# One hybrid decoder layer on one core: the page loop written out behind the q, k, v projection, pages in rings with a wait for each page, the memory projections moved into the loop's first chunks, and each prompt unit spread over three chunks

## What is computed

```python
def sb_block(z, mask, v, carry):
    log_om = jnp.where(mask, jax.nn.log_sigmoid(-z), 0.0)
    suffix = lax.cumsum(log_om, axis=3, reverse=True) - log_om + carry[..., None]
    a = jnp.where(mask, jnp.exp(jax.nn.log_sigmoid(z) + suffix), 0.0)
    o = jnp.einsum("bhqk,bkhd->bqhd", a, v.astype(jnp.float32))
    return o, carry + jnp.sum(log_om, axis=3)
...
    q, k, v, bg, u = mixer_inputs(yp, g_mix[l], w_in[l])
    attn = sb_attention_prompt(q, k, v, sb_bias[l])
    u_ext = jnp.pad(u, ((0, 0), (CONV_K - 1, 0), (0, 0)))
    yp = mixer_output(yp, attn, bg, causal_conv3(u_ext, w_conv[l]), g_attn_out[l], g_conv_out[l], w_out[l])
    mk, mv = memory_kv(mem_prompt, g_mem[l], w_ck[l], w_cv[l])
    yp = cross_attention(yp, mk, mv, g_ca[l], w_cq[l], w_co[l])
    yp = swiglu_ffn(yp, g_ffn[l], w_gate[l], w_up[l], w_down[l])
```

## Time and profile before

| | |
|---|---|
| median of 3 runs | 1239.15 us (1235.28 to 1242.31) |
| profiled execution | 1243.84 us, its span 1242.2 us |
| TensorE busy | 1117.2 us (90%) |
| VectorE, ScalarE, GpSimd busy | 629.9, 393.2, 405.8 us |
| HBM read, written | 206.18 MB, 5.80 MB |
| DMA queues of SP, GpSimd | 139.09 MB, 67.13 MB |

### The profile page before, as it was taken

The page is one execution under the profiler, slowest core; times in us unless marked ns, Lnnn a source line. Parts: engine busy times, 40 slices in busy tenths (PEclk is TensorE's granted clock), DMA queues, the critical chain, the costliest instruction groups (busy, mean ns, idle before and its releaser), DMA issues.

```text
span 1242.2 us, 27559 instructions
## 1 busy us (share of the span) xinstructions
PE 1117.2 (90%) x10055; PEld 1019.4 (82%) x10055; DVE 629.9 (51%) x890; ACT 393.2 (32%) x609; POOL 405.8 (33%) x327
## 2 busy tenths in 40 slices
PE   6999998789688888889789887899999999999997
PEld 5999997666466666666579865899999999999996
DVE  4214954555455554555579544954455001554444
ACT  6212123345354444445451344322121111211111
POOL 2333334243323333333333101342423334242331
PEclk8999999899899889899999999899999999999999
DMA  6222225899989989989954031322221332322222
GB/s 224 85 85 69 84 85 179 304 372 370 341 283 355 332 298 386 345 302 361 306 191 149 1 112 58 102 94 77 68 93 51 101 94 69 101 68 76 64 64 76
DMA packets 125012, 213.49 MB, mean 172 GB/s; under 512 B 9855, under 2 KB 68412, under 8 KB 124894
## 3 DMA queue, kind: packets, MB, share of 16 engines
q1 hardware_dynamic: 101962, 139.09, 33.4%
q0 software_dynamic: 20480, 67.13, 15.2%
q10 hardware_dynamic: 2452, 5.80, 1.3%
HBM read 206.18 MB, written 5.80 MB: 171 GB/s over the span
## 4 chain that ended last, share of the span: by engine, by line
PE 66%; SPq 10%; issue 7%; DMA 6%; DVE 6%; ACT 3%; POOL 1%; DVEq 0%; ACTq 0%; POOLq 0%
PE ps L460 50%; DMA k_page<-in_cache_sb_k 6%; SPq L562 5%; PE ps L1432 5%; SPq L568 4%; PE ps L526 4%; PE ps L301 2%; DVE h_lo L362 1%; DVE r_sum L623 1%; PE ps L1453 1%; POOL w_lo L415 1%; ACT prob L649 1%; DVE r_sq L618 1%; PE ps L1490 1%; DVE xT L613 0%
## 5 line engine op out<-in xcount | busy, mean ns | idle before, releaser
L415 POOL TENSOR_TENSOR w_lo<-w_raw,w_hi 128x2048 fp32r<-128x2048 f32 (+3 forms) x66 | 267.8, 4060 | 547.6 <-ACT w_hi L391 481.4
L460 PE MATMUL ps<-h_hi,w_hi 128*128 128x288 f32 x1216 | 264.8, 300 | 15.4 <-DVE h_lo L362 12.4
L460 PE MATMUL ps<-h_lo,w_hi 128*128 128x288 f32 x1216 | 263.2, 298 | 0.0
L460 PE MATMUL ps<-h_hi,w_lo 128*128 128x288 f32 x1216 | 262.6, 298 | 0.0
L568 POOL DMA_DIRECT2D v_page<-in_cache_sb_v x256 | 137.7, 538 | 260.7 <-issue 199.5
L391 ACT ACTIVATE w_hi<-w_raw 128x2048 fp32r<-128x2048 f32 (+3 forms) x62 | 106.5, 1721 | 365.2 <-PE ps L460 333.4
L460 PEld LDWEIGHTS ps<-h_hi,w_hi 128*128 128x128 f32 x1216 | 198.8, 192 | 17.1 <-issue 9.3
L460 PEld LDWEIGHTS ps<-h_lo,w_hi 128*128 128x128 f32 x1216 | 198.7, 191 | 0.0
L460 PEld LDWEIGHTS ps<-h_hi,w_lo 128*128 128x128 f32 x1216 | 198.5, 191 | 0.0
L1432 PE MATMUL ps<-cc,k_page 128*128 128x128 f32 x1024 | 145.2, 305 | 53.2 <-DMA k_page<-in_cache_sb_k 31.2
L1432 PEld LDWEIGHTS ps<-cc,k_page 128*128 128x128 f32 x1024 | 129.7, 157 | 69.1 <-DMA k_page<-in_cache_sb_k 35.1
(11 more groups left out here) (230 smaller groups left out, 1396.0 us busy)
## 6 DMA issues: line engine op xcount, KB each, us to landing
k_page<-in_cache_sb_k SPq DMA_DIRECT2D x256, 256.0 KB, 5.3
v_page<-in_cache_sb_v POOLq DMA_DIRECT2D x256, 256.0 KB, 5.4
w_raw<-in_w_in SPq DMA_DIRECT2D x12, 1024.0 KB, 5.1
w_raw<-in_w_gate SPq DMA_DIRECT2D x11, 1024.0 KB, 5.3
w_raw<-in_w_up SPq DMA_DIRECT2D x11, 1024.0 KB, 5.3
w_raw<-in_w_down SPq DMA_DIRECT2D x8, 768.0 KB, 4.4
w_raw<-in_w_down SPq DMA_DIRECT2D x8, 640.0 KB, 4.0
w_raw<-in_w_out SPq DMA_DIRECT2D x4, 1024.0 KB, 6.0
```

Source lines behind the costliest of these rows:

```text
L415: return nc.gpsimd.tensor_tensor(w_lo[s][:, ks, :], w_raw[s][:, ks, :], w_hi[s][:, ks, :].bitcast(F32), ALU.subtract)
L460: op = nc.tensor.matmul(ps[:, 2 * t + hf, 0:b - a], weights[s][:, k, t * P:(t + 1) * P], x[:, k0 + k, a:b], start=begin and k == ks[0] and ...
```

## The change

Five things change.

1. The groups are no longer a loop with a register but written out on every engine, so the copies of q, k and v to a fixed place go, and the operands are read where they lie.
2. K pages lie in one ring of 8 slots (16 before), V pages in one ring of 16. Every page load waits for the use of its own slot, and TensorE waits for two pages at a time.
3. The stages `ck` and `cv` go. K pages and the memory weights are loaded behind the last `in` weights. Memory product tiles 0 and 1 stand ahead of chunk 0, tiles 2 to 7 in chunks 0, 2 and 3, the row transposes of their results in chunk 4, and their stores on ScalarE's queue in chunk 4.
4. Prompt unit u has its scores in chunk u + 5, now behind the sample scores, and its transposes and sums two chunks later. The 16 units so lie in chunks 5 to 22.
5. The high and low parts of the conv half of the `out` operand get buffers of their own (`c_hi`, `c_lo`). They lie where two of the samples' memory V are loaded to, and SP waits for the last `out` tile before these loads.

```diff
-            for name in ("inb", "in", "ck", "cv"):
+            for name in ("inb", "in"):
                 load_stage(sp, name)
             sp.wait_ge(s_pt, 16)
...
-            with sp.Fori(0, GROUPS) as g:
-                for c in range(CP):
-                    load_pages(sp, g, c, ck, k_page, s_kp, s_ktr, 8)
-            sp.wait_ge(m_["pv"], 8 * GROUPS + 1)
+            def load_memory_weights(i):
+                if i < 2:
+                    sp.wait_ge(s_wlo, SLOT0["ck"] + i - 1)
+                else:
+                    sp.wait_ge(s_mem_tile, 2 * i - 2)
+                src = views["ck" if i < 2 else "cv"][:, :, (i % 2) * SLOTW:(i % 2 + 1) * SLOTW]
+                sp.dma_start(mw_raw[i % 2][:, :, :], src).then_inc(s_full[i % 2], 16)
+
+            k_pages(sp, 0)
+            load_memory_weights(0)
+            load_memory_weights(1)
+            for C in range(1, CHUNKS):
+                k_pages(sp, C)
+                if C in (1, 2):
+                    load_memory_weights(C + 1)
+            sp.wait_ge(s_mem_tile, 8)
+            sp.wait_ge(s_out, 16 * 5)
             load_stage(sp, "out")
...
             for b in range(BS):
                 load_mem(cmk, b, smk_tok[b]).then_inc(s_cmk, 16)
+            sp.wait_ge(s_tile["out"], 4 * PAIRS["out"])
             for b in range(2):
                 load_mem(cmv, b, smv_tok[b]).then_inc(s_cmv[0], 16)
             load_stage(sp, "cq")
```

The loads of pages (`k_pages` on SP, `v_pages` on GpSimd's queue):

```diff
+        def load_page(eng, C, q, cache, slot, loaded):
+
+            n = 64 * (C // 8) + 32 * (q // 4) + 28 - 4 * (C % 8) + q % 4
+            page = eng.value_load(ptb[0:1, n:n + 1], min_val=0, max_val=N_POOL - 1)
+            eng.dma_start(slot, cache[0, bass.ds(page, 1)].rearrange("o p h d -> p o (h d)")).then_inc(loaded, 16)
+
+        def k_pages(sp, C):
+
+            for q in range(8):
+                if C:
+                    sp.wait_ge(s_ktr, 8 * C + q - 7)
+                load_page(sp, C, q, ck, k_page[:, q:q + 1, :], s_kp[q // 2])
+
+        def v_pages(pool, C):
+
+            for q in range(8):
+                slot = 8 * (C % 2) + q
+                if C >= 2:
+                    pool.wait_ge(s_vsum, 8 * C + q - 15)
+                elif slot >= 11:
+                    pool.wait_ge(s_kv_out, 16 * 4)
+                load_page(pool, C, q, cv, v_page[:, slot:slot + 1, :], s_vp[slot // 2])
```

On ScalarE, VectorE and TensorE (P0 is 5):

```diff
             def group(g, last):
                 for c in range(8):
+                    C, u = 8 * g + c, 8 * g + c - P0
+                    sample_sigmoids(9 * g + c + 1, SEQ)
+                    if 3 <= u < 19 and c:
+                        prompt_out(u - 3)
+                    if C + 1 < CHUNKS:
+                        copy_k(C + 1)
+                    copy_weights(9 * g + c + 1, False)
+                    if 2 <= u < 18:
+                        copy_prompt_weights(u - 2)
+                    if 0 <= u < 16:
+                        prompt_sigmoids(u)
+                    if C in (0, 1):
+                        memory_hi(C + 2)
+                    if C == 4:
+                        memory_rows((0, 2, 4))
+                        store_memory()
...
+                    weights(9 * g + c + 1, 19 * g + 3 + 2 * c, SEQ)
+                    if C in (1, 3, 4):
+                        evac_memory((3, None, 5, 7)[C - 1])
+                    if C + 1 < CHUNKS:
+                        copy_k(C + 1)
...
+                    if 2 <= u < 18:
+                        copy_prompt_weights(u - 2)
+                    if 1 <= u < 17:
+                        prompt_weights(u - 1)
...
+                    if C + 1 < CHUNKS:
+                        k_transposes(C + 1)
+                    if C in (0, 2, 3):
+                        memory_tile((2, None, 4, 6)[C])
+                    if C == 4:
+                        memory_rows((0, 1))
+                    weight_transposes(9 * g + c + 1, 4, u - 2)
+                    if 2 <= u < 18:
+                        prompt_transposes(u - 2)
                     if c < 7:
-                        scores(g, c + 1)
+                        scores(C + 1)
                     elif not last:
-                        new_scores(g, 8)
-                    sums(g, c)
-                    if c % 2 == 1:
-                        prompt_sums(g, c // 2)
+                        new_scores(g + 1)
+                    if C in (0, 2, 3):
+                        memory_tile((3, None, 5, 7)[C])
+                    if C == 4:
+                        memory_rows((2, 3, 4))
+                    if 0 <= u < 16:
+                        prompt_scores(u)
+                    sums(C)
+                    if 2 <= u < 18:
+                        prompt_sums(u - 2)
```

More of the change, by code:

```diff
@@ new lines, in _ @@
+            split_stage(act, "in", between=lambda: tr_copy(act, even(U_M)), after=bias_and_memory)
+            copied(act, U_M[-1])
+            act.wait_ge(s_sum["conv"], 1)
+            hi_parts(act, "ck", mT, G_MEM, range(KD))
+            memory_hi(0)
+            memory_hi(1)
+            rms_root(act, "conv", rstd_c[:, :], T, CH)
+            nc.scalar.preload_act_table(ACT.Sigmoid)
+            tr_copy(act, even(U_VT))
+            tr_copy(act, even(U_KT))
+            copied(act, U_KT[-1])
@@ new lines, in group @@
+                    weights(9 * g + c + 1, 19 * g + 3 + 2 * c, SEQ)
[3 more added lines that the diff above has]
+                        copy_k(C + 1)
+                    if c == 7 and not last:
+                        queries(g + 1)
+                    if C in (0, 2, 3):
+                        evac_memory((2, None, 4, 6)[C])
+                    if C < 2:
+                        conv_root(C)
@@ L1279, in group @@
                         op = nc.vector.tensor_copy(
-                            pT[64 * h2:64 * h2 + 64, T_A:T_A + HP, bass.ds(g * 16 + (SEQ + 8 * s), 8)],
+                            pT[64 * h2:64 * h2 + 64, T_A:T_A + HP, SEQ + 16 * g + 8 * s:SEQ + 16 * g + 8 * s + 8],
                             rows[:, :, 16 * s + 8 * h2:16 * s + 8 * h2 + 8])
                 op.then_inc(m_["rows_copied"], 1)
-                if not last:
-                    fix_values(g, 8)
-            queries(0, 0)
-            fix_values(0, 0)
+            queries(0)
             weights(0, 0, NS)
-            copy_k(0, 0)
-            with dve.Fori(0, GROUPS - 1) as g:
-                group(g, False)
-            group(GROUPS - 1, True)
+            lo_parts(dve, "ck", mT, G_MEM, range(KD))
+            copy_k(0)
+            evac_memory(0)
+            evac_memory(1)
+            for g in range(GROUPS):
+                group(g, g == GROUPS - 1)
             grant(s_free["out"], 2)
@@ L1380, in _, with memory_tile @@
             tr_pe(pe, U_KT)
-            pe.wait_ge(s_op["ck"], KD)
-            gemm(pe, "ck", m_hi, m_lo, NMEM)
-            pe.wait_ge(s_evac["ck"], 1)
-            tr_pe(pe, U_MK[0:3])
-            gemm(pe, "cv", m_hi, m_lo, NMEM)
-            pe.wait_ge(s_evac["cv"], 1)
-            tr_pe(pe, U_MK[3:5])
-            def prompt_scores(g, qb):
-                if qb == 0:
-                    pe.wait_ge(p_["qk_fixed"], g * 2 + 2)
+            def memory_tile(j):
+                i, t = divmod(j, 2)
+                if t == 0:
+                    pe.wait_ge(s_wlo, SLOT0["ck"] + i + 1)
+                if j == 0:
+                    pe.wait_ge(s_op["ck"], KD)
+                    copied(pe, U_KT[-1])
+                if j == 1:
+                    pe.wait_ge(s_rt["conv"], 1)
+                if j >= 2:
+                    pe.wait_ge(s_mem_free, j - 1)
+                for k in range(KD):
+                    for w, (weights, x) in enumerate(((mw_hi, m_hi), (mw_hi, m_lo), (mw_lo, m_hi))):
+                        op = nc.tensor.matmul(ps[:, 5 + 2 * t, 0:NMEM], weights[i % 2][:, k, t * P:(t + 1) * P], x[:, k, :],
+                                              start=k == 0 and w == 0, stop=k == KD - 1 and w == 2)
+                op.then_inc(s_mem_tile, 1)
@@ L1520, in group @@
                 if not last:
-                    new_transposes(g, 8)
-                    scores(g, 8)
-                    new_sums(g, 8)
-            new_scores(0, 0)
-            k_transposes(0, 0)
-            new_transposes(0, 0)
-            scores(0, 0)
-            new_sums(0, 0)
-            with pe.Fori(0, GROUPS - 1) as g:
-                group(g, False)
-            group(GROUPS - 1, True)
-            pe.wait_ge(p_["out_copied"], 4 * GROUPS + 1)
+                    weight_transposes(9 * g + 9, 1, u - 1)
+                    scores(8 * g + 8)
+                    new_sums(g + 1)
+            new_scores(0)
+            k_transposes(0)
+            memory_tile(0)
+            copied(pe, U_KT[-1])
+            weight_transposes(0, 1, 0)
+            scores(0)
+            memory_tile(1)
+            new_sums(0)
+            for g in range(GROUPS):
+                group(g, g == GROUPS - 1)
+            pe.wait_ge(p_["out_copied"], 4 * GROUPS)
             gemm_out(pe)
```

494 lines of the change are left out of this document (234 added, 260 removed).

## The result

The kernel after takes **1260.2 us** (median of 4 runs, 1256.07 to 1261.32) and the kernel before 1240.63 beside it (4 runs). The ratio is 1.0162, 95% interval 1.0128 to 1.0197: slower by 1.6%, where 1228 us, faster, was forecast. The profiled execution took 1256.07 us (span 1254.4), 12.2 us more than the profiled execution of before.

What follows compares the result with a forecast made beforehand. DMA engines were taken as full for part of a group and starved otherwise, with TensorE stalled by late K copies. Terms -23.3 + 12.2 + 8.2 - 18.8 - 1.8 + 12 = -11.5: 1232 us profiled, 1228 median; own range 1215 to 1241, eight-in-ten 1197 to 1255.

Steps and rivals of the forecast that it cites:

- entry, to chunk 0: Ahead of the page loop: the first chunk is entered at 215 us instead of 238.5, -23.3 us.
- chunks 0 to 4: Start of the loop: six memory tiles and five row transposes but no prompt work, 62 us instead of 54.7.
- chunks 5 to 20, with the stores: Prompt work in each chunk and late K copies: 12.7 us a chunk, 212 against 204 us, plus 4.6 for stores.
- chunks 21 to 31: Mostly chunks without prompt work, pages loading at 387 GB/s: 108.5 us against 127.3, -18.8 us.
- tail of the loop: After chunk 31 no prompt unit is left to transpose and copy: -1.8 us.
- `cq` weights and all behind: Query weights' load stands behind the last output tile's wait on SP; TensorE sits 14 us and starts slow: +12 us.
- Rival 2: Eight-slot K ring too short, deciding from landings of 7.4 us on: slower, 1259 us or up to 1320; chance 0.18.
- Rival 1: Overlap works fully: chunks 5 to 20 take 10.9 us instead of 12.7, 29 us less, about 1199; chance 0.20.
- The sign I named for rival 2: Waits for k_page over 25 us in chunks 5 to 20 would show the prediction wrong.
- The stores: In chunk 5 ScalarE issues five stores before the sample sigmoids: 4.6 us charged with their waits.

Runs made afterwards that it cites:

- Experiment 3: The kernel after with 16 K page slots instead of 8 from chunk 6 on: ratio 1.0056 to the kernel before.
- Experiment 7: The kernel after without the 16 prompt attention units: 1249.36 us (ratio 1.0076 to before) with 8 K slots, 1214.84 us (0.9791) with 16 from chunk 6 on.
- experiment 6: The kernel after with prompt sigmoids behind the next chunk's sample sigmoids and 12 K slots from chunk 6 on: ratio 0.9857 to the kernel before.
- Experiment 11: The kernel after with cq weights first, 16 K slots, sigmoids behind, and the last two memory weight slots' low parts on VectorE instead of GpSimd: ratio 0.9758 to before.
- experiment 4: The kernel after (8 K slots) with ScalarE's prompt sigmoids moved behind the next chunk's sample sigmoids: ratio 1.0138 to the kernel before.
- experiment 5: The kernel after with both 16 K slots from chunk 6 on and prompt sigmoids behind the next sample sigmoids: 1221.88 us, ratio 0.9854 to the kernel before.
- experiment 8: The kernel after with the five memory row stores on SP behind chunk 6's K pages instead of on ScalarE in chunk 4: ratio 1.0173 to the kernel before.
- experiment 9: The kernel after with cq weights first, 16 K slots, sigmoids behind: 1209.85 us, ratio 0.9747 to before; with the five stores on SP too, 0.9746.
- experiment 2: The kernel before with only the wait for the last output tile put ahead of the memory V and cq weight loads: 1254.81 us, ratio 1.0102 to before.
- experiment 1: The kernel after with the cq weights' load put ahead of the wait for the last output tile on SP's queue: 1249.76 us, ratio 1.0043 to before.

## Why the prediction was wrong

By its own terms, with the profiled executions (before, after):

| term | predicted | measured |
|---|---|---|
| entry, to chunk 0 | -23.3 | -22.5 |
| chunks 0 to 4 | +7.6 | +16.1 |
| chunks 5 to 20, with the stores | +12.8 | +11.1 |
| chunks 21 to 31, to the end of the last sums | -18.8 | -4.1 |
| tail of the loop | -1.8 | -0.1 |
| `cq` weights and all behind | +12 | +11.7 |
| sum | -11.5 | +12.2 |

The forecast median was 32.5 us too low. 23.7 of them are in the table; the other 8.8 come from how the profiled execution stood to the median: 4.7 us above it before, 4.1 below it after. I had taken the same 4.7 off both. Two slips of arithmetic change nothing: 12.7 x 16 is 203.2, not 203.6, and 0.16 + 0.12 is 0.28, not 0.27.

**The step that failed is that of chunks 21 to 31**, "29.4 MB, at 387 GB/s 76 us": 14.7 us of the 23.7. The rate of the earlier trace rows had been reached with 16 K slots, and I carried it over to a ring of 8. Page waits in the second half of the transposes held these chunks to 353 GB/s (timeline of TensorE in after, chunk 26):

```profile
563.07 1.09 PE L1495 MATMUL ps<-cc,k_page 128*128 128x128 f32 x8 [1.14 <-DMA k_page<-in_cache_sb_k]
566.53 1.85 PE L1495 MATMUL ps<-cc,k_page 128*128 128x128 f32 x8 [2.36 <-DMA k_page<-in_cache_sb_k]
```

Experiment 3 shows how much of it is the ring: with 16 slots and nothing else changed these chunks take 113.0 us instead of 123.2, where 108.5 were predicted. That is 10.2 of the 14.7 us; for the other 4.5 no run has a cause. Experiment 7 shows the same of the ring without prompt work. **Rival 2 had the right mechanism** at 0.18 and came within about a microsecond of the time, 1259, but that is luck: its sum put the loss into chunks with landings of 10 us and more. The landing of a K page from 331 to 600 us was 5.9 us in the median with 8 slots and no prompt work, 11.4 at the longest. Its floor, 5.3 us plus the landing, is 11.2 us by the median; measured were 12.2, two group ends among them, and in single chunks anything from 9.3 to 17.3, so it is no floor for each chunk. The ring costs time at landings below the 7.4 us that I gave. As I read it, a chunk waits for the latest of its pages, and a ring without spare slots can't make a late page good; the lower clock behind each wait, which the sum did not have, comes on top. With 12 slots most of the waits are gone (experiment 6). The Trainium skill ("DMA: Bandwidth & Descriptors", Queues, rings and completion order) has each DMA engine go round-robin between the queues that have work for it. That was no reason against the rival: K and V landed equally fast (5.4 and 5.3 us in the page of after), and the loss comes from when a load may be issued, on which the rule is silent.

**Chunks 0 to 4, +8.4 us more than predicted.** Chunk 2 took 20.5 us instead of 15.4, chunk 1 10.1 instead of 8. I had no term for page waits among four loads of memory weights of 1 MB on the same queue, nor for the stopped scans, nor for the clock behind a wait. In chunk 2 of after TensorE waits 1.3 us for a page and 2.4 for a K copy that stands behind the stopped scan; from 247 to 253 the granted clock is then 0.53, and 16 transposes take 3.65 us where they take 2.03. Experiment 11 takes the stopped scans away and the time stays; page waits are what is seen in their place. That the weights' loads cause them was not tried, so this part stays argued.

**Chunks 5 to 20 were right** in time (216.6 us predicted with the stores, 215.1 measured), in the waits for the kT copies (22.5 us on VectorE and 4.2 on ScalarE between 286 and 500; some 30 predicted) and in their cause, which experiments 4 and 5 show. But they did not show what a cure is worth. Rival 1 gave 29 us for full overlap; with 8 slots the moved sigmoids were worth 0.002, with 16 slots 0.020 of the time, 25 us. The sign I named for rival 2, page waits over 25 us in these chunks, did not appear: the late copies hid the late pages. There were none between 286 and 500 us in after, and 13.9 us once the copies came earlier (experiment 4). It was a bad sign to name.

**The stores** were charged 4.6 us. Chunk 5 does last 15.1 us, with 4.2 us of waits, and with the stores off ScalarE and the long ring chunk 5 is 4.8 us shorter, so the charge was of the right size. On SP they cost as much again in late K pages (experiments 8, 9); whether another place would give it back is open.

**The tail** brought nothing: from the end of the last sums to the output product it is 3.75 us (3.86 before). The last weight transposes still wait 1.73 us and the group's rows still go through VectorE (1.39); so it seems that the removed prompt unit stood beside these; no run tests it.

**The `cq` weights** were right: gap 14 predicted, 15.6 measured, and by the ratios the time moved by 12.7 and 14.8 us in experiments 2 and 1. The landing was 7.3 us (685.69 to 693.01) for the 6.8 of the earlier trace rows.

## What to carry to other kernels

When one wait is shortened or hidden, ask which wait lies under it: neither TensorE's late copies nor the short ring showed its price alone (0.002 and 0.011), and the two edits together gave 0.031. Here 12 slots did what 16 did and 8 did not, at median landings of 5 to 6 us: size a ring by the lead time of its last slot against the latest landing, not the median, and don't carry a rate over that was measured with a deeper ring; leaving the work out altogether shows the floor at once. And a wait put into a DMA queue is paid by every load behind it: look at what stands there, and move it ahead.

## What the runs showed of the hardware

VectorE stood still while GpSimd subtracted. The scan took 4.49 and 4.34 us instead of 1.28, each time ending 1.08 us after GpSimd's instruction (226.80 + 4.59 = 231.39, scan to 232.47; 239.57 + 4.53 = 244.10, scan to 245.18; all in after). Each kernel above whose GpSimd makes these parts shows it (4.49 and 4.33 to 4.35 us; with eight V slots one scan of 5.46), and neither experiment 2 nor 11 does. The first `h_lo` ahead of the query product shows it too: issued 0.7 us after GpSimd's `w_lo`, it took 4.41 us instead of 0.81; where the `cq` weights come early and the two don't meet (experiment 1), two of them take 1.55 us. The kernel before has it as well. There a square of a 128x576 tile, 0.76 us by itself, began 0.45 us after the `w_lo` of 676.17 in the earlier trace rows (VectorE's timeline of before):

```profile
676.62 4.78 DVE L618 TENSOR_TENSOR r_sq<-xT 128x576 f32<-128x576 f32 x1
```

A copy out of PSUM (0.69 us, at 189.07) and a reciprocal of one tile (3.75, at 638.55) took beside a `w_lo` of before what they take alone. The Trainium skill ("SBUF — State Buffer", Who interferes with whom) says that a VectorE instruction with two SBUF inputs contends with a GpSimd instruction that reads SBUF and that the later one fully blocks. The rows agree: the scan reads two tiles, came 1.2 us after the subtraction and waited it out.

More slots made each page land later and the kernel faster: in experiment 7 the median landing of K pages from 331 to 500 us was 5.9 us with 8 slots and 12.5 and 13.1 in the two halves of the 16, at 333 and 386 GB/s.

Waits also took clock. In 331 to 400 us the granted clock was 0.88 of full speed in the kernel with 8 slots and no prompt work, where TensorE was busy 54.2 of 69 us, 0.92 with 16 slots and 60.0 us, and 1.00 with prompt work, 16 slots, the sigmoids behind and 68.8 us. Busy time alone does not order them: the kernel after was busy 58.9 us there and had 1.00; its longest stop was 1.9 us, those of the first two 2.3 and 2.1, for K pages.
